# One core: w_out taken by column halves across all token tiles, with each tile's transposes, squares and router logits split the same way and the expert buffers re-ordered

## The reference, cut to what matters

```python
x = x + merged @ w_out                       # 576 x 1024 times 1024 x 1024
xt = rmsnorm(x, norm2_g)
g_logits = xt @ w_rg + b_rg                  # 4 expert groups
e_logits = xt @ w_rexp + b_rexp              # 8 experts in each
# top-1 group, top-2 experts inside it, weights w
for e in range(32):
    h = silu(xt @ w_e_gate[e]) * (xt @ w_e_up[e])
    y = y + combine[:, e:e+1] * (h @ w_e_down[e])
x = x + y;  final rmsnorm
```

## Time and profile before

| what | value |
|---|---|
| three runs | 781.94, 782.52, 783.98 us (median 782.52) |
| profiled execution, its span | 783.6 us; the page gives no other time for it |
| PE busy | 741.4 us (95%) |
| DVE, ACT, POOL busy | 408.8, 259.2, 74.4 us |
| moved by DMA | 190.68 MB, mean 243 GB/s |
| chain that ended last | PE 76%, DMA 14%, DVE 5%, ACT 3% |
| first expert product starts | 536.4 us |
| last expert weight chunk in | about 752 us |

### The profile page before, as it was taken

How to read it: one execution, slowest core, us unless ns; L and a number is a source line. 1 busy time by engine, 2 the same in 40 slices (tenths; PEclk the granted TensorE clock), 3 DMA queues, 4 the chain that set the end, 5 groups by cost and what they waited for, 6 DMA issues and landing times.

```text
span 783.6 us, 12757 instructions
## 1 busy us (share of the span) xinstructions
PE 741.4 (95%) x5288; PEld 576.0 (74%) x5288; DVE 408.8 (52%) x755; ACT 259.2 (33%) x446; POOL 74.4 (9%) x104
## 2 busy tenths in 40 slices
PE   8999999999999999999999999999999997778884
PEld 7999999999999777899999988885333332323322
DVE  6999839986347785665154386554112111114226
ACT  5662351123486645532442341230111111100113
POOL 0100022001011111000000000011121221111100
PEclk9999999999999999999999999999999999999997
DMA  9578326434238433400260694389999999999994
GB/s 342 202 264 316 109 82 106 118 115 151 102 131 323 162 138 118 182 1 2 108 219 12 222 425 189 128 353 345 419 423 424 418 424 424 419 423 425 422 388 161
DMA packets 38143, 190.68 MB, mean 243 GB/s; under 512 B 5914, under 2 KB 7466, under 8 KB 21864
## 3 DMA queue, kind: packets, MB, share of 16 engines
q1 hardware_dynamic: 23696, 148.22, 47.8%
q0 software_dynamic: 11200, 34.98, 13.4%
q10 hardware_dynamic: 3184, 6.60, 2.3%
HBM read 176.17 MB, written 21.41 MB: 252 GB/s over the span
## 4 chain that ended last, share of the span: by engine, by line
PE 76%; DMA 14%; DVE 5%; ACT 3%; issue 1%; SPq 1%; DVEq 0%; ACTq 0%; POOLq 0%
PE ps L662 72%; DMA sb<-in_wexp 11%; PE ps L676 4%; DMA expert_rows<-sb 2%; DVE sb L2763 1%; DMA sb<-expert_rows 1%; DMA sb<-in_xT 1%; DVE sb L2298 1%; DVE sb L2284 1%; SPq L562 1%; ACT sb L1431 1%; ACT sb L1631 1%; DVE sb L2696 0%; ACT sb L1653 0%; ACT sb L1636 0%
## 5 line engine op out<-in xcount | busy, mean ns | idle before, releaser
L662 PE MATMUL ps<-sr 128*128 128x288 f32 (+3 forms) x2906 | 407.3, 300 | 3.5 <-DVE ps L2701 3.0
L662 PEld LDWEIGHTS ps<-sr 128*128 128x128 f32 (+1 forms) x2906 | 388.1, 188 | 18.6 <-issue 5.6
L662 PE MATMUL ps<-sb 128*64 128x512 f32 (+16 forms) x1984 | 296.9, 429 | 28.7 <-DMA sb<-in_wexp 18.1
L662 PEld LDWEIGHTS ps<-sb 128*64 128x64 f32 (+7 forms) x1984 | 148.0, 148 | 149.8 <-issue 124.7
L2632 DVE SCALAR_TENSOR_TENSOR sb<-sb,ps 128x256 f32<-128x256 f32 x16 | 6.7, 421 | 117.7 <-ACT sb L1830 117.7
L676 PEld LDWEIGHTS ps<-sb 128*128 128x128 f32 (+3 forms) x398 | 42.2, 140 | 31.0 <-issue 28.6
L676 PE MATMUL ps<-sb 128*128 128x128 f32 (+3 forms) x398 | 53.7, 273 | 2.3 <-issue 1.4
L2246 DVE TENSOR_TENSOR sr<-sb,sr 128x2048 fp32r<-128x2048 f32 (+1 forms) x17 | 39.3, 2320 | 29.1 <-ACT sr L1545 19.0
L2640 DVE COPY sb<-ps 128x1024 f32<-128x1024 f32 x15 | 18.4, 1225 | 54.5 <-PE ps L662 54.5
L1431 ACT ACTIVATE sb<-ps 128x576 f32<-128x576 f32 (+3 forms) x28 | 21.9, 783 | 67.4 <-PE ps L662 47.4
L2357 DVE SCALAR_TENSOR_TENSOR sb<-sb,ps 128x576 f32<-128x576 f32 x24 | 18.1, 753 | 46.5 <-PE ps L662 46.3
(11 more groups left out here) (291 smaller groups left out, 509.2 us busy)
## 6 DMA issues: line engine op xcount, KB each, us to landing
sb<-in_wexp SPq DMA_DIRECT2D x91, 1024.0 KB, 22.1
sb<-in_wstream SPq DMA_DIRECT2D x33, 1024.0 KB, 5.7
expert_rows<-sb ACTq DMA_DIRECT2D x1, 4608.0 KB, 24.9
sb<-in_mkT POOLq DMA_DIRECT2D x8, 512.0 KB, 7.7
sb<-in_mv POOLq DMA_DIRECT2D x8, 512.0 KB, 5.1
sb<-expert_rows SPq DMA_DIRECT2D x4, 1024.0 KB, 9.0
sb<-in_wexp SPq DMA_DIRECT2D x5, 768.0 KB, 25.4
sb<-in_x SPq DMA_DIRECT2D x4, 512.0 KB, 14.1
```

Source lines behind the costliest of these rows:

```text
L662: return signed(nc.tensor.matmul(*a, **kw))
```

## The change

PE now takes w_out's column blocks 0 and 1 for all tiles (`w01`, `w11`, `w02`, `w03`, `w04`) and then blocks 2 and 3 for all tiles, two blocks at a time for tile 1 too. A tile's first 512 columns are transposed, copied, squared and multiplied into the logits before its second 512 columns exist (`xa`, first half; `xb`, second half); these pieces stand between parts of the second half's products. The square of a half goes to a buffer of its own (`M_SQ`), and the first half's sum, scaled, is the bias of the root of the whole (`first_square`, `second_square`). PSUM buffers of the jobs behind `w04` are written out by hand (`plan_pairs`). Chunks 8 to 11 take the buffers of blocks 0 and 1 and are issued when `w04` is done; 12, 13 and 14 take the sums' buffers of tiles 1, 2 and 3 behind `w21`, `w22` and `w23`; 15 to 18 take the buffers of blocks 2 and 3 behind `w24`. On DVE `norm(t)` moves one round back, behind `select_first(t)` of the next round, so that `norm(3)` comes behind the last `add_h`. On PE `table(3)` moves behind `ranks(4)`.

```diff
+def w_out_slots(b):
+    return [straight(a) for a in (raw_at(NBLOCKS - 4 + b), raw_at(NBLOCKS - 3 + b), HI_AT["w", b], HI_AT["w", b + 1])]
+
+
+SLOTS_E += w_out_slots(0)
 SLOTS_E += [straight(24320), straight(O_A + 16640), [(27648, ((1280, 2), (1, 1024)), 0, 2048)]]
-SLOTS_E += [straight(a) for b in (0, 2) for a in (raw_at(NBLOCKS - 4 + b), raw_at(NBLOCKS - 3 + b), HI_AT["w", b], HI_AT["w", b + 1])]
+SLOTS_E += w_out_slots(2)
...
-    jobs += ["w00", "w20"]
-    for t in range(1, TT):
-        if t == 1:
-            jobs += ["w01", "w11", "x2T0", "w21", "lg0", "w31", "rk0"]
-            continue
-        jobs += [f"x2T{t - 1}", f"w0{t}", f"tb{t - 2}", f"lg{t - 1}", f"w2{t}", f"rk{t - 1}"]
-    jobs += ["x2T4", "xs", "lg4", "tb3", "rk4", "xs2", "tb4", "cnt"]
+    jobs += ["w00", "w20", "w01", "w11", "x2T0", "w02", "lg0", "w03", "rk0", "xa1", "w04"]
+    jobs += ["xa2", "w21"]
+    for t in range(2, TT):
+        jobs += [f"xb{t - 1}", f"tb{t - 2}", f"lg{t - 1}"] + ([f"xa{t + 1}"] if t + 1 < TT else []) + [f"rk{t - 1}", f"w2{t}"]
+    jobs += ["xb4", "lg4", "rk4", "tb3", "xs", "tb4", "cnt"]
...
+def plan_pairs():
+
+    pairs = {job: i % 4 for job, i in J.items() if i <= J["w04"]}
+    one, two, turned, logit = pairs["w03"], pairs["w04"], pairs["xa1"], pairs["rk0"]
+    assert sorted((one, two, turned, logit)) == list(range(4))
+    for t in range(1, TT):
+        pairs[f"w2{t}"] = pairs[f"xb{t}"] = pairs[f"rk{t}"] = one if t % 2 else two
+        pairs[f"lg{t}"] = logit
+    for job in ("xa2", "xa3", "xa4", "tb0", "tb1", "tb2", "xs"):
+        pairs[job] = turned
+    pairs.update(tb3=one, tb4=one, cnt=logit)
+    return pairs
+
+
+PAIR = plan_pairs()
+NTH = {job: sum(PAIR[other] == PAIR[job] for other in J if J[other] < J[job]) for job in J}
+TURNED = ["x2T0", "xa1", "xa2", "xb1", "xa3", "xb2", "xa4", "xb3", "xb4"]
...
+        def first_h(t):
+
+            return 4 + 2 * t
+
+        def all_h(t):
+
+            return 12 + 2 * t if t else 4
...
             filled(sp, "w20")
             main_chunk(7)
-            for n, job in ((8, "w31"), (9, "w22"), (10, "w23")):
+            filled(sp, "w04")
+            for n in range(8, 12):
+                main_chunk(n)
+            for n, job in ((12, "w21"), (13, "w22"), (14, "w23")):
                 filled(sp, job)
                 main_chunk(n)
-            sp.wait_ge(w_used, NBLOCKS - 2)
-            for n in range(11, 15):
-                main_chunk(n)
-            sp.wait_ge(w_used, NBLOCKS)
+            filled(sp, "w24")
             for n in range(15, 19):
...
-            def turn_norm(t):
+            def turn_h(job, t, kts):
+
                 R = WROWS[t]
-                pe.wait_ge(h_ready, 4 * (t + 1))
-                take(f"x2T{t}")
-                for kt in range(KT):
-                    last = turn_tile(pat(pair(f"x2T{t}"), kt * 128, (1, R)),
+                pe.wait_ge(h_ready, first_h(t) if kts[-1] < KT - 1 else all_h(t))
+                take(job)
+                for kt in kts:
+                    last = turn_tile(pat(pair(job), kt * 128, (1, R)),
                                      at(H_AT[t] + kt * 128, (1, 128), pn=R), at(O_ID, (1, R), pn=R))
                 last.then_inc(ps_ready, 1)
 
-            def logits(t):
+            def logits(t, turned, kts):
+
                 R = WROWS[t]
-                pe.wait_ge(x2T_sb, t + 1)
+                pe.wait_ge(x2T_sb, TURNED.index(turned) + 1)
                 if t == 0:
                     pe.wait_ge(wr_ready, 1)
-                take(f"lg{t}")
-                for kt in range(KT):
+                if kts[0] == 0:
+                    take(f"lg{t}")
+                for kt in kts:
                     last = mm(pat(pair(f"lg{t}"), 0, (1, 40), pn=R), at(M_X2T + (t % 2) * 1024 + kt * 128, (1, R)),
                               at(M_WR + kt * 40, (1, 40)), start=(kt == 0), stop=(kt == KT - 1))
-                last.then_inc(ps_ready, 1)
+                if kts[-1] == KT - 1:
...
+            low_half, high_half = range(4), range(4, KT)
+            one_block(0)
+            one_block(1)
+            turn_h("x2T0", 0, range(KT))
+            two_blocks(0, 2)
+            logits(0, "x2T0", range(KT))
+            two_blocks(0, 3)
             ranks(0)
+            turn_h("xa1", 1, low_half)
+            two_blocks(0, 4)
+
+            pe.wait_ge(lo_ready, LOWS.index(("w", 3)) + 1)
+            two_blocks(2, 1, range(3))
+            turn_h("xa2", 2, low_half)
+            two_blocks(2, 1, range(3, 6))
+            logits(1, "xa1", low_half)
+            two_blocks(2, 1, range(6, KT))
             for t in range(2, TT):
-                for b in (0, 2):
-                    job = f"w{b}{t}"
-                    take(job)
-                    for kt in range(KT):
-                        if b == 0 and kt == 5:
-                            turn_norm(t - 1)
-                        last = three(pat(pair(job), 0, (1, 512)), sum_at(t, kt, 1), sum_at(t, kt, 0),
-                                     HI_AT["w", b] + kt * 256, w_out[b] + kt * 256, kt == 0, kt == KT - 1, 256,
-                                     (HI_AT["w", b + 1] - HI_AT["w", b], w_out[b + 1] - w_out[b]))
-                    last.then_inc(ps_ready, 1)
-                    if t == TT - 1:
-                        owed.append((w_used, 2))
-                    if b == 0:
-                        table(t - 2)
-                        logits(t - 1)
+                two_blocks(2, t, range(2))
+                turn_h(f"xb{t - 1}", t - 1, high_half)
+                table(t - 2)
+                two_blocks(2, t, range(2, 3))
+                logits(t - 1, f"xb{t - 1}", high_half)
+                if t + 1 < TT:
+                    turn_h(f"xa{t + 1}", t + 1, low_half)
+                two_blocks(2, t, range(3, 5))
+                logits(t, f"xa{t}", low_half)
+                two_blocks(2, t, range(5, 7))
                 ranks(t - 1)
+                two_blocks(2, t, range(7, KT))
...
-            first_rows(0, range(2))
-            turn_norm(4)
-            first_rows(0, range(2, KT))
-            logits(4)
-            table(3)
+            first_rows(0, low_half)
+            turn_h("xb4", 4, high_half)
+            first_rows(0, high_half)
+            logits(4, "xb4", high_half)
             first_rows(1)
             first_rows(2)
             ranks(4)
+            table(3)
             first_rows(3)
             first_rows(4)
             table(4)
...
-            def copy_x2T(t):
-                R = WROWS[t]
-                if t >= 2:
+            def copy_turned(job, t, kts):
+
+                R, first, many = WROWS[t], kts[0], len(kts)
+                if t >= 2 and first == 0:
                     filled(act, f"lg{t - 2}")
-                copy_out(f"x2T{t}", at(M_X2T + (t % 2) * 1024, (128, KT), (1, R)),
-                         pat(pair(f"x2T{t}"), 0, (128, KT), (1, R)), x2T_sb)
+                copy_out(job, at(M_X2T + (t % 2) * 1024 + first * 128, (128, many), (1, R)),
+                         pat(pair(job), first * 128, (128, many), (1, R)), x2T_sb)
...
-            for t in range(TT):
+            def square(t, first, n, total):
+
                 R = WROWS[t]
-                if t == 0:
-                    shift(0)
-                    shift(2)
-                else:
-                    copy_x2T(t - 1)
-                if t == TT - 1:
-                    copy_x2T(t)
-                act.wait_ge(h_ready, 4 * (t + 1))
-                ss, spare = at(R_SS + t, (1, 1), pn=R), 1 if t == TT - 1 else t % 2
-                if t >= 2:
-                    act.wait_ge(x2_out[spare], 16 * (2 if t == TT - 1 else t // 2))
-                fn(at(M_X2 + spare * 1024, (1, D), pn=R), at(H_AT[t], (1, D), pn=R), ACT.Square, accum_out=ss).then_inc(squares, 1)
-                act.wait_ge(squares, TT + 3 + t)
-                fn(ss, ss, ACT.Sqrt, scale=1.0 / D, bias=at(O_EPS, (1, 1), pn=R)).then_inc(rt_ready, 1)
+                c_squares[0] += 1
+                fn(at(M_SQ, (1, n), pn=R), at(H_AT[t] + first, (1, n), pn=R), ACT.Square,
+                   accum_out=at(total, (1, 1), pn=R)).then_inc(squares, 1)
+                act.wait_ge(squares, c_squares[0])
+
+            def root(t, **bias):
+                ss = at(R_SS + t, (1, 1), pn=WROWS[t])
+                fn(ss, ss, ACT.Sqrt, scale=1.0 / D, **bias).then_inc(rt_ready, 1)
+
+            def first_square(t):
+
+                act.wait_ge(h_ready, first_h(t))
+                square(t, 0, D // 2, R_SA + t)
+                part = at(R_SA + t, (1, 1), pn=WROWS[t])
+                fn(part, part, ACT.Identity, scale=1.0 / D, bias=at(O_EPS, (1, 1), pn=WROWS[t])).then_inc(half_root, 1)
+
+            def second_square(t):
+                act.wait_ge(h_ready, all_h(t))
+                square(t, D // 2, D // 2, R_SS + t)
+                act.wait_ge(half_root, t)
+                root(t, bias=at(R_SA + t, (1, 1), pn=WROWS[t]))
+
+            c_squares = [TT + 2]
```

(52 more changed lines are left out.)

42 lines of the change are left out of this document (25 added, 17 removed).

## The result

The changed kernel takes 790.51 us (median of four executions, 789.14 to 791.43), the kernel before, on the same chip, 782.38 (781.94 to 783.98): a ratio of 1.0086, 95% interval 1.0072 to 1.0101. It is slower by 0.86%, outside my range. (The quotient of the two medians alone is 1.0104; the ratio with its interval is what I go by.)

What follows compares the result with a forecast made beforehand. DMA's weight stream bounds the kernel once unbroken; X changes nothing, and the earlier R closes a DMA hole, taken as 0.7 us: 783.6 - 0.7 = 782.9 for the profiled execution, or 781.8 from 782.52. Range 779.8 to 784.5.

Steps and rivals of the forecast that it cites:

- X: Issue of weight chunk 19, when the last store of normed rows has landed; forecast 535.2 us, as before.
- R: First return of a weight buffer, after the first expert product, releasing chunk 20; forecast 538.9 us, 1.2 us earlier.
- the plateau: Stretch from about 546 us where DMA streams 76 chunks and row traffic at 422 GB/s, said to set the pace.
- the byte sum: Chunks 15 to 18 take 10 us, two row stores 2.5, latency 1.2: everything in at 535.0.
- Rival 3: Slower: last store takes its full 8.5 us, lands at 537.1; 783.8, or 785.3 with round cover gone; chance 0.17.
- Rival 2: Last row store lands early, X 532 to 534, R 538.0 to 538.5, no clock fall: 779.5 to 780.9; chance 0.25.
- The round-robin rule: DMA engines serve queues packet by packet, so a store beside one loaded queue gets about half the rate, landing at 533.6.
- the 8.5 us row: Profile row before the change: a row store took 8.5 us under weight chunks, against 2.9 alone.
- w24's end: End of PE's w24 product, forecast 521.2 us for 520.0 before, with chunks 15 to 18 going out at 521.3.
- the collision on POOL: POOL's multiplication of tile 4, 524.9 to 527.2, delays DVE's choose(4); one-hot at 528.8, bounds 527.1 and 529.3.
- the rounds: PE's second-half products with pieces between them: 8.9 us a round, new waits costed at nothing, tightest cover 0.7 us.
- The clock: PE's granted clock, expected to fall again in the tail behind w24, costing 1.7 us (bounds 1 and 2.5).

Runs made afterwards that it cites:

- run 1: The kernel before, unchanged, profiled a second time: 783.5 us, ratio 0.9998.
- run 3: Changed kernel, with chunk 20 and all behind it waiting until the first gather has landed: 788.3 us, ratio 1.0057 to before.
- run 7: Changed kernel with norm(3) early, and chunk 20 and all behind it waiting until the first gather has landed: 785.25 us, ratio 1.0018 to before.
- run 16: Changed kernel with norm(3) early, chunk 20 issued when the second of four pieces of gate_up(0, 1) is done: 784.99 us, ratio 1.0008 to before.
- run 18: Changed kernel with norm(3) early, chunk 20 issued when the first of four pieces of gate_up(0, 1) is done: 783.99 us, ratio 1.0007 to before.
- Run 4: Kernel before, with one wait added so POOL issues the first gather only at the first return of buffers: 790.34 us, ratio 1.0083.
- run 14: Changed kernel with norm(3) early, chunks 17 and 18 issued behind the wait for the row stores: 786.57 us, ratio 1.0037 to before.
- run 15: Changed kernel, norm(3) left in place, chunks 17 and 18 issued behind the wait for the row stores: 786.61 us, ratio 1.0041 to before.
- run 6: Changed kernel with norm(3) moved ahead of place_rows(3) in the last round: 787.81 us, ratio 1.0055 to before.
- run 17: Changed kernel, norm(3) left in place, chunk 20 issued when the second of four pieces of gate_up(0, 1) is done: 786.92 us, ratio 1.0059 to before.
- run 12: Kernel before, with norm(3) moved behind the last add: 793.29 us, ratio 1.0126.
- run 13: Changed kernel with norm(3) early, chunk 18 issued behind the wait for the row stores: 787.88 us, ratio 1.0051 to before.
- run 5: Kernel before, with the last row store held until the first half of the first pair's rows is copied out: 791.72 us, ratio 1.0091.
- run 10: Changed kernel with norm(3) early, chunk 20 waiting for a semaphore POOL raises behind its second gather: 787.85 us, ratio 1.0048 to before.
- run 11: Changed kernel, norm(3) left in place, chunk 20 waiting for a semaphore POOL raises behind its second gather: 791.13 us, ratio 1.0094 to before.

## Why the prediction was wrong

**The step that failed** is the sum's claim that the end moves with "the moment from which the weight stream is unbroken, and by nothing else", that only X and R set this moment, and that the rest of the plateau is DMA's "whatever PE does meanwhile". At the plateau's start all 20 buffers are full, and each chunk goes out only when PE returns one; PE's next steps need the first gather. That gather was in the sum only as bytes (one of "the first two gathers, 0.5 MB each"), with neither a landing nor a waiter. (The bytes were too many as well: POOL's queue moved 0.22 MB for the first gather in before and run 1, and 0.46 MB for both in runs 3, 7, 16 and 18.) It waits for the last store, goes out 0.3 us ahead of chunks 20 and 21, and lands 8.3 us later where it took 3.5 in before. Run 4 shows that this alone, with X as in before, costs 0.83%.

**X as the sole measure is refuted.** Run 4 has X where before has it, runs 14 and 15 have it 1.9 and 1.3 us earlier (all from A), and they are 0.83, 0.37 and 0.41% slower. Runs 6, 16 and 18 have the same X, 77.4, and 1.0055, 1.0008 and 1.0007: they differ only in when chunk 20 goes out. Whether the 79.5 us of after cost something beside the gather isn't settled. No run with X at 79.4 or later is level with before; run 17, with the gather mended, is still 0.59% slower.

What goes with the time is the third return. Against run 1 it is 7.8 us later in after, of which 4.7 are standstill, 2.2 the slow clock and 0.9 the later R. The results' load is then 6.7 later and the span's end 7.4. From third return to load it is 200.7 to 202.3 us in the twelve profiles with a gap of 2.86 us or more, with a filled one, or with the whole tail late (run 12), so there the stream hangs on PE's returns. In the other eight it is 201.4 to 204.8, the most in runs 3, 7 and 16, where chunk 20 waited longest: there the hole in DMA counts too. From the load to the end of the span it is another 29.9 to 32.8 us (30.4 in run 1, 32.8 in run 14, 31.1 in after), a scatter that no run explains.

**X was also mis-sized, 537.9 for 535.2.** Two terms. The store was issued at 529.94, not 528.6: POOL's multiplication began 0.8 us later than forecast (525.72 to 528.09, with a TENSOR_SCALAR of choose(4) of 1.77 us under it), ACT's scaling began 0.4 us behind its end and took 1.15, and the issue came 0.3 us behind that. And the byte sum, everything in at 535.0, was short at both ends. The bytes started slowly (DMA's share was 0.51 and 0.79 in the two us from 522) and ran until about 536.3 (0.94 in 535 to 536, 0.29 in the next us, 0.02 in 537 to 538), and the landing came at 537.9. In run 13 they ended near 534.2, and the store landed at 536.1. The prediction's own sign of being wrong fired here: a last store that lands outside 534 to 537. The landing follows the last byte by some 1.6 to 1.9 us.

**The rivals.** Rival 3 named the place (last store late by its full 8.5 us at 537.1) and the mechanism up to X. Its price, one us per us of X less 0.6, gave 783.8 and missed the gather behind the store. Rival 2 missed the gather too: run 15's store takes 3.8 us and X is 533.8, and the kernel is 0.41% slower, though there two chunks stand beside the gather that rival 2 would have had ahead of the store. The round-robin rule that was weighed against the 8.5 us row (the Trainium skill, DMA: Bandwidth & Descriptors, Queues, rings and completion order) would have given about 5 us for the store by the prediction's estimate. Beside three or four chunks the last store took 7.9 to 9.3 us. The trace bears the rule out all the same, counted in packets: from 531 to 534 in before each of the two queues (q1 is SP's, q0 is POOL's) moved 114.

```profile
q1 hardware_dynamic: 114, 0.80, 63.9%
q0 software_dynamic: 114, 0.47, 37.8%
```

But POOL's held 0.47 MB and SP's 0.80, so the store got 0.37 of the bytes and not half. And the estimate left out a late start. The store issued at 526.66 moved its first byte about 3.8 us later, where run 5's, issued beside nothing at 534.90, had it after about 1.1 and landed in 2.9. The prediction read its 8.5 us row as speaking against the rule, and in packets it doesn't. What delays the first byte no run shows.

**What was right.** w24's end (521.56 for 521.3; from A chunk 15 is 1.4 us later than in before, in every profile of either kind, where the sum had 1.2), R by its number (539.13 for 538.9), the collision on POOL, the rounds (PE busy 80.18 of 81 us from 455 to 536, no gap of weight), and DMA's plateau from 640 on. The clock did not fall in the tail: 1.00 at 526 where it was 0.59. It fell there in three of the five profiles of before and its variants (before, runs 5 and 12, not runs 1 and 4) and in none of the fifteen of after and its variants. Its price of 1.7 us was right, for from POOL's multiplication to R it is 19.0 us with it (521.04 to 540.08) and 17.4 in run 1 (522.33 to 539.74). Without the fall R was to be 538.3; the one-hot came at 529.4 instead of 528.8, and R at 539.13. The middle value was hit by two errors that cancel, and the 1.2 us gained at R were not gained: against run 1, where the clock didn't fall either, R is 0.9 us later.

**How the two met.** Chunks 20 and 21 are released by R and the gather by the last store. Against run 1 (from A) the change moved R back by 0.9 us and the gather by 2.7; against the first profile of before, with its late R, it moved R forward by 0.7 and the gather back by 1.1. Either way the distance shrinks from 2.1 us to 0.3. Two events that I priced apart met in one queue. Norm(3)'s place is 2.4 us of the loss by run 6 against after, 3.6 by run 10 against run 11. The order of the gather and chunk 20 gives back 0.27% alone (run 17) and 0.47% once norm(3) is early (run 16 against run 6). With both mended 0.07 to 0.08% is left, within what a measurement tells from none. So the two parts aren't separate sums: each helps more when the other is mended.

**What stays open.** Why the gather takes what it takes is described here, not explained: no run changes the queues' service itself. The profile's bytes by queue say where the time goes. The first byte on POOL's queue came some 1.75 us behind the gather's issue in before, 3.0 in runs 3, 7, 16, 17 and 18, and 3.75 in after. From there to the landing it was 1.75, 1.6 to 1.7, and 4.6 us. So both the start and the transfer are longer beside more chunks, the transfer most of all; how the queues share the bytes stands above under the rivals. The spread of run 17 isn't resolved, nor why a clear distance didn't help runs 14 and 15, beyond that three chunks were in flight there when the gather was issued. And the loss has three sizes: 8.1 us by the medians, 6.7 by the ratio, 7.4 by the two profiles from A. They agree only within the scatter.
